# Low parts of the hidden activations of chunks 1 to 3 of both feed-forward layers: written by GpSimd where VectorE wrote them

## The chip, the cores and the metric

The kernel runs on one core of one Trainium2 chip. Its time is the device time of one execution in microseconds (us). Three executions of the kernel before took 1832.42 us in the median (1831.35 to 1832.48). TensorE is called PE in the rows, its weight load PEld, VectorE DVE, ScalarE ACT, GpSimd POOL and the queue that issues the transfers SP.

## The reference

Two blocks follow each other on an activation of 512 tokens by 1024 features in float32: a stick-breaking attention layer and an MLA layer, then an even mixer, a feed-forward layer, a differential attention mixer, a feed-forward layer and a last norm. Of it all, only the feed-forward layers (`L` = 0 and 1) are touched:

```python
def sq_relu_mlp(h, w_up, w_down):
    u = jnp.einsum('btd,df->btf', h, w_up)
    return jnp.einsum('btf,fd->btd', jnp.square(jax.nn.relu(u)), w_down)

for layer in range(DEPTH):            # DEPTH = 2
    ...
    h = h + sq_relu_mlp(rms_norm_2(h, mlp_norm_g[layer]), mlp_w_up[layer], mlp_w_down[layer])
```

Here `w_up` is 1024 by 4096 and `w_down` 4096 by 1024.

## The kernel before

**High and low parts.** Every float32 operand of a matrix product is split in two: a high part, a rounded copy (type fp32r) made by ScalarE, and a low part, the operand minus its high part. A product is then three matmuls: high by high, low by high, high by low. For the weights of ordinary blocks `WH` is the high and `WL` the low part (L269 and L278) of what landed in `WRAW`, which has 2 buffers (`WH` and `WL` have 3). For the hidden activations of a feed-forward layer they are `HIDH` and `HIDL`.

**Four chunks.** A feed-forward layer goes over the 4096 hidden features in four chunks `c` of 1024. In each chunk the up product makes 8 planes of 128 features by 512 tokens, and the down product multiplies them by 8 blocks of `w_down` (`m`), each into its own PSUM bank, and VectorE adds the bank to `X` (L516). Chunk 0 is made in the ordinary way; its low parts are written by GpSimd (L2574, in `mlp_gpsimd`).

**Chunks 1 to 3.** Their up products use Strassen-like block products: 7 half-size products (P1 to P7) instead of 8. One chunk has 4 pairs `p` (two planes of features `p` and `p + 4`), each pair has two halves, which gives 8 slots of 42 matmuls of 256 columns (L2402, L2404, L2405, `fast_pe`). For each slot VectorE forms sums of weight blocks (`fast_sums`, L2331 to L2336), ScalarE the high parts (`fast_high`, L2344) and VectorE the low parts (`fast_low`, L2349) in `G`. When a pair's products are there, ScalarE copies P1 out (`first_act`), VectorE joins the seven products in the one buffer `Q` (`join_first`, L2424, L2428, L2431; `join_last`, L2437), ScalarE takes relu, square and high part (`relu_act`, L2443, L2445, L2447: 128 by 1024 into `HIDH`), and then the low part is made, `HIDL` = `Q` - `HIDH`, 128 by 1024 (`hid_low`, L2451), by VectorE.

**Who waits for the low part.** `join_first` of the next pair writes `Q` again, and so waits for `hid_low` of the pair before. The down product waits for the high and the low part of a plane before its first matmul. It starts with blocks `m` = 0 and 1 on the 6 planes of pairs 0 to 2, and only then takes the planes of pair 3, for both:

```python
ks = (0, 4, 1, 5, 2, 6, 3, 7) if c else tuple(range(8))
...
for m in range(2):
    down(c, m, ks[0:6])
for m in range(2):
    down(c, m, ks[6:8])
```

**What sets the order.** Each engine runs its own hand-written program in order, and semaphores link them. In `mlp_vector` a chunk is a loop of 9 steps `i`, in which the work of several functions is interleaved; `mlp_scalar` has the same loop. The SP queue's order is planned; a load of a weight block into `WRAW` waits for the low part of the block two before, and a load for `fast_sums` waits for the `fast_low` of the slot three before.

Of the kernel before, what the change touches and what calls it, by code (L numbers as in the profile page):

```python
# [45 lines left out]
class Counts:  # L46
# [11 lines left out]
    def inc(self, sem, *keys):  # L58

        self.n[sem] = self.n.get(sem, 0) + 1  # L60
        for key in keys:
            assert self.table.get(key, (sem, self.n[sem])) == (sem, self.n[sem]), (key, sem)
            self.table[key] = (sem, self.n[sem])
        return self.sems.get(sem), 1

    def at(self, *key):

        if not self.sems:
            return None, 0
        sem, n = self.table[key]  # L70
        return self.sems[sem], n
# [65 lines left out]
def program(nc, A, out):  # L137
    ctx = ExitStack()
    with ctx:
# [131 lines left out]
        def split_low(e, w, b, pool):  # L271
            if b >= len(stream) or (b in on_pool) != pool:
                return
            n = stream[b][2]
            if b >= NS:
                w.wait_ge(*at("used", b - NS))
            w.wait_ge(*at("high", b))
            e.tensor_tensor(WL[b % NS][:, 0:n], WRAW[b % NR][:, 0:n], WH[b % NS][:, 0:n].bitcast(F32),  # L278
                            ALU.subtract).then_inc(*inc("s_low_pool" if pool else "s_low", ("low", b)))
# [10 lines left out]
        def after_block(name, m=0):  # L290

            return block[name, m] + NS
# [176 lines left out]
        def factor_vec(e, w, g):  # L469
            s = TMP[:, 1, :]  # L470
            w.wait_ge(*at("sum", g))
            e.tensor_scalar(s, banks["sum", g], 1.0 / DM, EPS, ALU.mult, ALU.add).then_inc(*inc("s_newton", ("mean", g)))
            if g in rn_of:
                w.wait_ge(*at("token sum", g))
                e.tensor_scalar(RN2[:, :], banks["token sum", g][:, 0:NT], 1.0 / DM, EPS, ALU.mult, ALU.add).then_inc(
                    *inc("s_newton", ("token mean", g)))
            w.wait_ge(*at("mean", g))
            w.wait_ge(*at("guess", g))
            newton(e, w, g, "newton", s, RS[:, :], "rs")
# [34 lines left out]
        def add_x(e, w, name, m):  # L514
            w.wait_ge(*at("tile", name, m))
            e.tensor_tensor(X[:, m, :], X[:, m, :], banks[name, m], ALU.add).then_inc(  # L516
                *inc("s_evac", ("evac", name, m)))
# [501 lines left out]
        for h in range(L1_HEADS):  # L1019
            p = halves[h % 2]  # L1020
# [1287 lines left out]
        def flat(x):  # L2308
            return x.rearrange("p s n -> p (s n)")
# [18 lines left out]
        def fast_sums(e, w, L, s):  # L2328
            w.wait_ge(*dma(f"s_raw{s % 3}", L * NF // 3 + s // 3 + 1))
            a21, a11, a12, a22, s1, s3, s2, s4 = (raw_part(s, i) for i in range(8))  # L2330
            e.tensor_tensor(s1, a21, a22, ALU.add).then_inc(*inc("s_fast_sum", ("first sum", L, s)))  # L2331
            e.tensor_tensor(s3, a21, a11, ALU.subtract).then_inc(*inc("s_fast_sum", ("third sum", L, s)))
            w.wait_ge(*at("first sum", L, s))
            e.tensor_tensor(s2, s1, a11, ALU.subtract).then_inc(*inc("s_fast_sum", ("second sum", L, s)))
            w.wait_ge(*at("second sum", L, s))
            e.tensor_tensor(s4, a12, s2, ALU.subtract).then_inc(*inc("s_fast_sum", ("sums", L, s)))  # L2336
# [10 lines left out]
        def fast_low(e, w, L, s):  # L2347
            w.wait_ge(*at("fast high", L, s))
            e.tensor_tensor(flat(G[s % 3][:, 7:14, :]), raw_part(s, 1, 7), flat(G[s % 3][:, 0:7, :]).bitcast(F32),  # L2349
                            ALU.subtract).then_inc(*inc("s_fast_low", ("fast low", L, s)))  # L2350

        def stage_vec(e, w, L, p):
            g = f"mlp{L}"
            w.wait_ge(*at("rs", g))
            for i, k in ((6, p), (4, p + 4)):
                made = e.scalar_tensor_tensor(out=flat(STAGE[p][:, i:i + 2, :]), in0=X[:, k, :], scalar=gain(g)[:, k:k + 1],
                                              in1=RS[:, :], op0=ALU.mult, op1=ALU.mult)
                made.then_inc(*inc("s_staged", *[("plane staged", L, p)] * (i == 4)))

        def plane_mix(e, w, L, p):  # L2360
            S = STAGE[p]
            w.wait_ge(*at("plane staged", L, p))
            e.tensor_tensor(S[:, 0:2, :], S[:, 7:8, :].broadcast_to([128, 2, 256]), S[:, 5:7, :], ALU.subtract).then_inc(
                *inc("s_mixed", ("first mix", L, p)))
            w.wait_ge(*at("first mix", L, p))
            e.tensor_tensor(S[:, 2, :], S[:, 5, :], S[:, 1, :], ALU.subtract).then_inc(
                *inc("s_mixed", ("second mix", L, p)))
            w.wait_ge(*at("second mix", L, p))
            e.tensor_tensor(S[:, 3, :], S[:, 4, :], S[:, 2, :], ALU.subtract).then_inc(*inc("s_mixed", ("mixed", L, p)))
# [64 lines left out]
        def join_last(e, w, L, c, pair):  # L2434
            key = (L, c, pair)
            w.wait_ge(*at("product", *key, "P4"))
            e.tensor_tensor(Q[:, 0:4:3, :], Q[:, 5:7, :], pair_bank(pair, 3), ALU.add).then_inc(  # L2437
                *inc("s_joined", ("joined", *key, 3)))
# [10 lines left out]
        def hid_low(e, w, L, c, p):  # L2449
            w.wait_ge(*at("hid hi", L, c, p))  # L2450
            e.tensor_tensor(flat(HIDL[:, 4 * p:4 * p + 4, :]), flat(Q[:, 0:4, :]),  # L2451
                            flat(HIDH[:, 4 * p:4 * p + 4, :]).bitcast(F32), ALU.subtract).then_inc(
                *inc("s_fast_hid_lo", ("hid lo", L, c, p)))
# [36 lines left out]
        def mlp_vector(e, w, L):  # L2490
            g = f"mlp{L}"
            for m in range(8):
                if m == 0:
                    factor_vec(e, w, g)
                w.wait_ge(*at("tile", ("up", L, 0), m))
                if m > 3:
                    w.wait_ge(*at("hid lo", L, 0, m - 4))
                e.scalar_tensor_tensor(out=TMP[:, m % 4, :], in0=banks[("up", L, 0), m], scalar=0.0, in1=RS[:, :],
                                       op0=ALU.max, op1=ALU.mult).then_inc(*inc("s_evac", ("evac", ("up", L, 0), m)))
                split_low(e, w, after_block(("up", L, 0), m), False)  # L2500
                if 0 < m < 5:
                    stage_vec(e, w, L, m - 1)
            for c in range(4):
                first = 8 * c
                if c:
                    for i in range(9):
                        s = first - 8 + i
                        if i and not i % 2:
                            join_last(e, w, L, c, i // 2 - 1)
                        if 0 < i < 6:  # L2510
                            fast_low(e, w, L, s + 2)
                        if i < 5:
                            fast_sums(e, w, L, s + 3)
                        if i > 5:
                            split_low(e, w, block[("dn", L, c), i - 6], False)
                        if i and not i % 2:
                            hid_low(e, w, L, c, i // 2 - 1)
                        if i % 2:
                            join_first(e, w, L, c, i // 2)
                if c == 3:  # L2520
                    break
                for m in range(8):
                    add_x(e, w, ("dn", L, c), m)
                    if m < 5:
                        split_low(e, w, after_block(("dn", L, c), m), False)
                    if c == 0 and m < 4:
                        plane_low(e, w, L, m)
                    if m > 4:
                        fast_low(e, w, L, first + m - 5)
                    if 3 < m < 7:  # L2530
                        fast_sums(e, w, L, first + m - 4)
            if L == 0:
                close_vec(e, w, ("dn", 0, 3), "mix1")
# [37 lines left out]
        def mlp_gpsimd(e, w, L):  # L2571
            for m in range(8):
                w.wait_ge(*at("hid hi", L, 0, m))
                e.tensor_tensor(hid_plane(m, 1), TMP[:, m % 4, :], hid_plane(m, 0).bitcast(F32),  # L2574
                                ALU.subtract).then_inc(*inc("s_hid_lo", ("hid lo", L, 0, m)))
                if m > 3:
                    plane_mix(e, w, L, m - 4)


        o_slots = [slot for b in range(4) for slot in (("o_q", 2 * b), ("o_k", 2 * b), ("o_q", 2 * b + 1),  # L2580
# [945 lines left out]
```

## Time and profile before

| | |
|---|---|
| median of 3 executions | 1832.42 us (1831.35 to 1832.48) |
| profiled execution, its own time | 1835.86 us |
| its span in the trace | 1834.0 us |
| busy: PE, DVE, ACT, POOL | 98%, 63%, 47%, 25% of the span |
| granted TensorE clock, mean | 0.995 |
| chain of work that ended last | 85% PE, 6% DVE, 4% ACT, 2% POOL |

The shares of busy time are averages over all layers. The chain that ended last is followed back from the last instruction, at each step to what released it; its share by engine says which engine set the end. The stages of interest are the chunks 1 to 3 of the two feed-forward layers, at 968.7 to 1220 us and at 1570.5 to 1822 us of the span. A row of the timeline gives start, duration, engine, line, operation, output and inputs, and in brackets the idle time of its engine before it and who ended it. A row's duration holds a start-up that overlaps the end of the instruction before it, so two rows of one engine overlap a little.

### The profile page before, as it was taken

How to read it: one execution, taken by the hardware profiler on the slowest of the kernel's cores; microseconds unless marked ns; L12 is line 12 of the kernel's file. 1: busy time of each engine (PE TensorE's matmuls, PEld its weight loads, DVE VectorE, ACT ScalarE, POOL GpSimd, SP SyncE). 2: the span in 40 equal slices, each digit the busy share in tenths (PEclk: the TensorE clock that was granted, in tenths of full speed). 3: DMA queues.
4: the chain of work that ended last, by engine and by line, in shares of the span. 5: the costliest groups of instructions: out<-in, count | busy, mean ns of one | idle time of the engine just before them, and what ended most of it. 6: DMA issues, size and time to landing. Idle time of an engine off the chain costs nothing.

```text
span 1834.0 us, 26208 instructions
## 1 busy us (share of the span) xinstructions
PE 1789.8 (98%) x10340; PEld 1460.4 (80%) x10340; DVE 1150.3 (63%) x1861; ACT 866.9 (47%) x1409; POOL 450.9 (25%) x451
## 2 busy tenths in 40 slices
PE   7999999999999999999999999999999999999997
PEld 6877777775678757677879898988888787989896
DVE  5355556575546688854578575765677657858574
ACT  5236665455435465564345252633445434435253
POOL 0035551101311235560140000005678214000000
PEclk9999999999999999999999999999999999999999
DMA  5321111231013411111232322222222123232322
GB/s 177 101 78 49 47 47 58 80 101 50 24 47 100 133 60 34 36 36 58 80 122 86 115 93 104 93 97 83 84 88 76 46 81 127 81 115 92 106 91 80
DMA packets 44521, 149.20 MB, mean 81 GB/s; under 512 B 6000, under 2 KB 6384, under 8 KB 44400
## 3 DMA queue, kind: packets, MB, share of 16 engines
q1 hardware_dynamic: 44400, 147.53, 24.1%
q8 instruction: 83, 1.36, 0.3%
q14 instruction: 38, 0.31, 0.1%
HBM read 139.64 MB, written 2.10 MB: 77 GB/s over the span
## 4 chain that ended last, share of the span: by engine, by line
PE 85%; DVE 6%; ACT 4%; POOL 2%; issue 2%; DMA 1%; POOLq 0%; SPq 0%; DVEq 0%; ACTq 0%
PE BANK L301 18%; PE BANK L303 17%; PE BANK L302 17%; PE BANK L2405 4%; PE BANK L2404 4%; PE BANK L2402 4%; PE BANK L955 3%; PE BANK L688 2%; PE BANK L1739 1%; PE BANK L1720 1%; DMA WRAW<-in_wc 1%; DVE WL L278 1%; PE BANK L1696 1%; PE BANK L1012 1%; PE BANK L2710 1%
## 5 line engine op out<-in xcount | busy, mean ns | idle before, releaser
L269 ACT ACTIVATE WH<-WRAW 128x1024 fp32r<-128x1024 f32 (+1 forms) x214 | 223.0, 1044 | 340.8 <-PE BANK L303 306.0
L278 DVE TENSOR_TENSOR WL<-WRAW,WH 128x1024 fp32r<-128x1024 f32 (+1 forms) x201 | 256.3, 1276 | 138.8 <-ACT WH L269 138.6
L301 PE MATMUL BANK<-HH,WH 128*128 128x512 f32 x664 | 273.1, 411 | 12.1 <-DVE WL L278 9.8
L303 PE MATMUL BANK<-HL,WH 128*128 128x512 f32 x664 | 260.2, 392 | 0.0
L302 PE MATMUL BANK<-HH,WL 128*128 128x512 f32 x664 | 259.9, 391 | 0.0
L301 PE MATMUL BANK<-HIDH,WH 128*128 128x512 f32 (+1 forms) x520 | 201.2, 387 | 1.6 <-issue 1.5
L302 PE MATMUL BANK<-HIDH,WL 128*128 128x512 f32 (+1 forms) x520 | 200.7, 386 | 0.0
L303 PE MATMUL BANK<-HIDL,WH 128*128 128x512 f32 (+1 forms) x520 | 200.7, 386 | 0.0
L2405 PE MATMUL BANK<-HP,G 128*128 128x256 f32 x672 | 190.2, 283 | 0.0
L2404 PE MATMUL BANK<-HP,G 128*128 128x256 f32 x672 | 190.2, 283 | 0.0
L2402 PE MATMUL BANK<-HP,G 128*128 128x256 f32 x672 | 190.1, 283 | 0.0
L516 DVE TENSOR_TENSOR X<-X,BANK 128x512 f32<-128x512 f32 x95 | 65.2, 686 | 167.9 <-PE BANK L303 167.7
L301 PEld LDWEIGHTS BANK<-HH,WH 128*128 128x128 f32 x664 | 125.5, 189 | 46.6 <-issue 22.5
L303 PEld LDWEIGHTS BANK<-HL,WH 128*128 128x128 f32 x664 | 125.2, 189 | 27.1
L302 PEld LDWEIGHTS BANK<-HH,WL 128*128 128x128 f32 x664 | 125.6, 189 | 25.6 <-issue 2.9
L2404 PEld LDWEIGHTS BANK<-HP,G 128*128 128x128 f32 x672 | 129.0, 192 | 0.2
L2402 PEld LDWEIGHTS BANK<-HP,G 128*128 128x128 f32 x672 | 129.0, 192 | 0.2
L2405 PEld LDWEIGHTS BANK<-HP,G 128*128 128x128 f32 x672 | 129.0, 192 | 0.0
L301 PEld LDWEIGHTS BANK<-HIDH,WH 128*128 128x128 f32 x520 | 97.7, 188 | 22.6 <-issue 3.2
L303 PEld LDWEIGHTS BANK<-HIDL,WH 128*128 128x128 f32 x520 | 97.7, 188 | 19.8
L302 PEld LDWEIGHTS BANK<-HIDH,WL 128*128 128x128 f32 x520 | 97.7, 188 | 19.4
L2344 ACT ACTIVATE G<-RAW 128x1792 fp32r<-128x1792 f32 x32 | 54.5, 1703 | 88.3 <-DVE RAW L2336 68.7
(446 smaller groups left out, 3694.2 us busy)
## 6 DMA issues: line engine op xcount, KB each, us to landing
WRAW<-in_w SPq DMA_DIRECT2D x77, 512.0 KB, 3.5
WRAW<-in_wd SPq DMA_DIRECT2D x64, 512.0 KB, 3.5
RAW<-in_wf SPq DMA_DIRECT2D x32, 512.0 KB, 3.6
WRAW<-in_wu SPq DMA_DIRECT2D x16, 512.0 KB, 3.5
TMP<-in_wf SPq DMA_DIRECT2D x16, 512.0 KB, 3.5
WRAW<-in_w0o SPq DMA_DIRECT2D x8, 512.0 KB, 3.5
WRAW<-in_w1o SPq DMA_DIRECT2D x8, 512.0 KB, 3.4
WRAW<-in_wc SPq DMA_DIRECT2D x8, 512.0 KB, 3.5
```

Of the source, the lines that this page charges most:

```text
L269: e.activation(WH[b % NS][:, 0:n], WRAW[b % NR][:, 0:n], ACT.Copy).then_inc(*inc("s_high", ("high", b)))
L278: e.tensor_tensor(WL[b % NS][:, 0:n], WRAW[b % NR][:, 0:n], WH[b % NS][:, 0:n].bitcast(F32), ALU.subtract).then_inc(*inc("s_low_pool" if p ...
L301: e.matmul(dst, ah, bh, start=first and i == 0, stop=False)
L302: e.matmul(dst, al, bh, start=False, stop=False)
L303: made = e.matmul(dst, ah, bl, start=False, stop=last and i == len(sets) - 1)
L516: e.tensor_tensor(X[:, m, :], X[:, m, :], banks[name, m], ALU.add).then_inc(*inc("s_evac", ("evac", name, m)))
L688: made = e.matmul(l0_bank(h, bk)[:, c0 + 128 * (jj - j):c0 + size[j]], ntri if jj == j else nones, nlf[:, h % 2, col[jj]:col[jj] + size[jj ...
L955: made = e.matmul(bank[:, c], a, b, start=(i == 0), stop=(i == len(sets) - 1), skip_group_check=True)
L2344: e.activation(flat(G[s % 3][:, 0:7, :]), raw_part(s, 1, 7), ACT.Copy).then_inc(*inc("s_fast_high", ("fast high", L, s)))
L2402: e.matmul(dst, wh[:, a, cols], hi, start=half == 0 and j not in started, stop=False, skip_group_check=True)
L2404: e.matmul(dst, wl[:, a, cols], hi, start=False, stop=False, skip_group_check=True)
L2405: made = e.matmul(dst, wh[:, a, cols], lo, start=False, stop=half == 1 and i == 1, skip_group_check=True)
```

## The change

`hid_low` is called from `mlp_gpsimd` instead of `mlp_vector`. The function is the same, with the same wait and the same semaphore, and the low part is the same subtraction of 128 by 1024 elements. 24 instructions move: 2 layers, 3 chunks, 4 pairs.

```diff
@@ mlp_vector: loop over the 9 steps i of a chunk
                         if i > 5:
                             split_low(e, w, block[("dn", L, c), i - 6], False)
-                        if i and not i % 2:
-                            hid_low(e, w, L, c, i // 2 - 1)
                         if i % 2:
                             join_first(e, w, L, c, i // 2)
@@ mlp_gpsimd: behind the loop over chunk 0
                 if m > 3:
                     plane_mix(e, w, L, m - 4)
+            for c in range(1, 4):
+                for p in range(4):
+                    hid_low(e, w, L, c, p)
```

On VectorE, at pair 0 of chunk 1 of layer 0, the program's order changes like this (difference of before and after; L2334 and L2336 are the last sums of a slot, L2349 the `fast_low` of the next):

```order
 L2334 TENSOR_TENSOR TMP<-TMP 128x256
 L2336 TENSOR_TENSOR TMP<-TMP 128x256
-L2451 TENSOR_TENSOR HIDL<-Q,HIDH 128x1024
 L2349 TENSOR_TENSOR G<-TMP,G 128x1792
 L2331 TENSOR_TENSOR RAW<-RAW 128x256
```

The `hid_low` between them is gone, and `fast_low` follows the sums.

On VectorE, at the end of the same chunk (pairs 2 and 3), before; L278 is the low part of a block of the down weights:

```order
L2437 TENSOR_TENSOR Q<-Q,BANK 128x2x256
L278 TENSOR_TENSOR WL<-WRAW,WH 128x1024
L2451 TENSOR_TENSOR HIDL<-Q,HIDH 128x1024
L278 TENSOR_TENSOR WL<-WRAW,WH 128x1024
L2424 TENSOR_TENSOR Q<-Q,BANK 128x2x256
L2428 TENSOR_TENSOR Q<-Q,BANK 128x512
L2431 TENSOR_TENSOR Q<-Q,BANK 128x256
L2437 TENSOR_TENSOR Q<-Q,BANK 128x2x256
L278 TENSOR_TENSOR WL<-WRAW,WH 128x1024
L2451 TENSOR_TENSOR HIDL<-Q,HIDH 128x1024
L516 TENSOR_TENSOR X<-X,BANK 128x512
```

and in the changed kernel:

```order
L2437 TENSOR_TENSOR Q<-Q,BANK 128x2x256
L278 TENSOR_TENSOR WL<-WRAW,WH 128x1024 x2
L2424 TENSOR_TENSOR Q<-Q,BANK 128x2x256
L2428 TENSOR_TENSOR Q<-Q,BANK 128x512
L2431 TENSOR_TENSOR Q<-Q,BANK 128x256
L2437 TENSOR_TENSOR Q<-Q,BANK 128x2x256
L278 TENSOR_TENSOR WL<-WRAW,WH 128x1024
L516 TENSOR_TENSOR X<-X,BANK 128x512
```

The `hid_low` of pair 2 stood between two weight splits, and that of pair 3 was the last of the chunk; both are gone from VectorE.

On GpSimd, behind the last `plane_mix` (L2363 to L2369) of layer 0, where the next work was that of the attention layer after it (L3091, one line later in the changed kernel):

```order
L2363 TENSOR_TENSOR STAGE<-STAGE 128x512
L2366 TENSOR_TENSOR STAGE<-STAGE 128x256
L2369 TENSOR_TENSOR STAGE<-STAGE 128x256
L2451 TENSOR_TENSOR HIDL<-Q,HIDH 128x1024 x12
L3092 TENSOR_TENSOR TMP<-TMP,ROPE 128x512
L3099 TENSOR_TENSOR OS<-TMP,OS 128x512
```

The 12 instructions of a layer stand in a row in GpSimd's program, with nothing of its other work between them.

## Rows read from the trace of the kernel before

**Rows 1.** Stretches: length, busy (count) of PE PEld DVE ACT POOL, clock, DMA, GB/s
```profile
968.70:1009.10 40.40, 40.40 (x338) 40.36 (x338) 33.27 (x46) 22.73 (x22) 0.00 (x0) 1.00 0.24 81
...
1738.20:1822.00 83.80, 83.80 (x547) 77.09 (x547) 52.14 (x69) 37.32 (x41) 0.00 (x0) 1.00 0.20 70
```

**Rows 2.** Groups of instructions by line and form: busy us, mean ns, idle before
```profile
L2451 DVE TENSOR_TENSOR HIDL<-Q,HIDH 128x1024 fp32r<-128x1024 f32 x24 | 29.4, 1224 | 26.1 <-ACT HIDH L2447 26.1
...
L278 POOL TENSOR_TENSOR WL<-WRAW,WH 128x1024 fp32r<-128x1024 f32 x6 | 14.3, 2390 | 4.2 <-ACT WH L269 4.2
```

**Rows 3.** Timeline of VectorE, chunk 1 of layer 0
```profile
985.04 1.22 DVE L2451 TENSOR_TENSOR HIDL<-Q,HIDH 128x1024 fp32r<-128x1024 f32 x1
986.89 2.03 DVE L2349 TENSOR_TENSOR G<-TMP,G 128x1792 fp32r<-128x1792 f32 x1 [0.63 <-ACT G L2344]
...
997.99 2.03 DVE L2349 TENSOR_TENSOR G<-RAW,G 128x1792 fp32r<-128x1792 f32 x1 [0.63 <-ACT G L2344]
...
1005.77 1.23 DVE L2451 TENSOR_TENSOR HIDL<-Q,HIDH 128x1024 fp32r<-128x1024 f32 x1 [2.18 <-ACT HIDH L2447]
1006.91 1.22 DVE L278 TENSOR_TENSOR WL<-WRAW,WH 128x1024 fp32r<-128x1024 f32 x1
1008.04 0.68 DVE L2424 TENSOR_TENSOR Q<-Q,BANK 128x512 f32<-128x512 f32 x1
...
1013.89 1.23 DVE L2451 TENSOR_TENSOR HIDL<-Q,HIDH 128x1024 fp32r<-128x1024 f32 x1 [2.18 <-ACT HIDH L2447]
```

**Rows 4.** Timeline of ScalarE, chunk 1 of layer 0
```profile
983.93 1.06 ACT L2447 ACTIVATE HIDH<-Q 128x1024 fp32r<-128x1024 f32 x1
...
1002.49 1.06 ACT L2443 ACTIVATE Q<-Q 128x1024 f32<-128x1024 f32 x1 [3.32 <-DVE Q L2437]
...
1012.79 1.06 ACT L2447 ACTIVATE HIDH<-Q 128x1024 fp32r<-128x1024 f32 x1
```

**Rows 5.** Timeline of TensorE: first plane and first plane of pair 3, down product
```profile
1009.07 0.40 PE L301 MATMUL BANK<-HIDH,WH 128*128 128x512 f32 x1
...
1017.25 0.39 PE L301 MATMUL BANK<-HIDH,WH 128*128 128x512 f32 x1
```

**Rows 6.** Timeline, chunk 3 of layer 1: low part of pair 3, its first matmul
```profile
1783.51 1.23 DVE L2451 TENSOR_TENSOR HIDL<-Q,HIDH 128x1024 fp32r<-128x1024 f32 x1 [2.18 <-ACT HIDH L2447]
...
1786.74 0.39 PE L301 MATMUL BANK<-HIDH,WH 128*128 128x512 f32 x1
```

**Rows 7.** Timeline, GpSimd and VectorE on two SBUF inputs at the same time
```profile
926.72 1.29 POOL L2574 TENSOR_TENSOR HIDL<-TMP,HIDH 128x512 fp32r<-128x512 f32 x1
...
926.88 2.21 DVE L278 TENSOR_TENSOR WL<-WRAW,WH 128x1024 fp32r<-128x1024 f32 x1 [2.31 <-ACT WH L269]
...
936.27 1.66 POOL L2369 TENSOR_TENSOR STAGE<-STAGE 128x256 f32<-128x256 f32 x1
...
937.25 2.57 DVE L2380 TENSOR_TENSOR HP<-STAGE,HP 128x1792 fp32r<-128x1792 f32 x1
...
1304.49 2.35 POOL L3098 TENSOR_TENSOR OS<-TMP,OS 128x512 fp32r<-128x512 f32 x1
...
1304.49 1.21 DVE L278 TENSOR_TENSOR WL<-WRAW,WH 128x1024 fp32r<-128x1024 f32 x1
```

**Rows 8.** Timeline: who starts how long after whom, and GpSimd's 128 by 1024
```profile
892.12 0.63 ACT L2544 ACTIVATE HIDH<-TMP 128x512 fp32r<-128x512 f32 x1
...
892.84 1.30 POOL L2574 TENSOR_TENSOR HIDL<-TMP,HIDH 128x512 fp32r<-128x512 f32 x1 [55.70 <-ACT HIDH L2544]
...
149.77 0.74 POOL L920 TENSOR_TENSOR LH<-SCR,LH 128x256 fp32r<-128x256 f32 x1 [0.23 <-DVE LH L798]
...
150.56 0.73 PE L688 MATMUL BANK<-LH,TRI 128*128 128x512 f32 x2 [0.32 <-POOL LH L920]
...
1279.26 2.37 POOL L278 TENSOR_TENSOR WL<-WRAW,WH 128x1024 fp32r<-128x1024 f32 x1
```

**Rows 9.** The page's transfer issues: KB each, median us to landing
```profile
WRAW<-in_wd SPq DMA_DIRECT2D x64, 512.0 KB, 3.5
```

## Prediction

> **What bounds the kernel now.** I read the busy time by stretch first. In the first block-product stretch of chunk 1 TensorE is busy for all of its 40.40 us at the full clock, and in the last one, chunk 3 of layer 1 with its down product, for all of its 83.80 us, while GpSimd does nothing in either [rows 1]. So in these chunks TensorE alone sets the time: relief of VectorE gives nothing back, and the change can only cost where it makes TensorE wait. The groups then give the sizes: the 24 `hid_low` take 1.22 us each on VectorE, and the nearest GpSimd operation, the same subtraction of 128 by 1024 with the same types, takes 2.39 us in the mean [rows 2], 2.37 where nothing stands in its way [rows 8].
>
> The timelines show the margins. VectorE runs `hid_low` of pair 0 at 985.04, then waits 0.63 us for ScalarE's high part before `fast_low` at 986.89; 11.10 us later, at 997.99, stands the same picture for pair 1. `hid_low` of pair 2 starts at 1005.77, a weight split (L278) follows at 1006.91 and `join_first` of pair 3 right behind it at 1008.04; `hid_low` of pair 3 starts at 1013.89 [rows 3]. In between ScalarE waits for VectorE (3.32 us before the relu of pair 2) and takes three passes of 1.06 us; the high part of pair 3 is ready at 1012.79 + 1.06 = 1013.85 [rows 4]. TensorE starts the down product at 1009.07 and comes to the first plane of pair 3 after 36 matmuls, at 1017.25 [rows 5]. That is the only deadline that is near: the low part of pair 3 is ready at 1013.89 + 1.23 = 1015.12, 2.13 us before. The six chunks repeat this within 0.02 us (start of `hid_low` to deadline 3.36 us), but for the last, with 3.23 us [rows 6].
>
> **The change, step by step.** *Removed:* 24 times 1.2 us on VectorE. At pairs 0 and 1 this frees nothing, since `fast_low` behind it waits for ScalarE, whose order does not change; the 1.2 us turn into waiting. At pairs 2 and 3 VectorE waits for ScalarE's high part anyway. Worth to TensorE: 0.
>
> *Added on GpSimd:* 2.37 us in place of 1.22. It starts 892.84 - (892.12 + 0.63) = 0.09 us after ScalarE's end, where VectorE took 1013.89 - 1013.85 = 0.04, and TensorE starts 150.56 - (149.77 + 0.74) = 0.05 us after a GpSimd end [rows 3, 4, 8]. By itself: 1013.85 + 0.09 + 2.37 + 0.05 = 1016.36, still 0.89 us ahead of 1017.25. Nothing on GpSimd's queue waits behind it: it is idle in these stretches [rows 1].
>
> *What it does to VectorE.* The trace has cases of both engines subtracting SBUF tensors at once [rows 7]. GpSimd's L2574 ran from 926.72 to 928.01; VectorE's split, started at 926.88, took 2.21 us, not 1.22, and ended at 929.09, 1.08 us after GpSimd. GpSimd's L2369 ended at 937.93; VectorE's L2380, 128 by 1792 like `fast_low`, took 2.57 us and ended at 939.82, 1.89 us after. The other way round, GpSimd's L3098 at 1304.49, beside a VectorE split that kept its 1.21 us, took 2.35 us in place of about 1.3. So of two such operations the later one stands still until the first has ended, and then needs 1.08 us (split) or 1.89 us (`fast_low`). `hid_low`, the splits and `fast_low` all read two SBUF tensors. With that:
> - Pair 0: high part ready at 983.93 + 1.06 = 984.99; GpSimd from 985.08 to 987.45. `fast_low` wants 986.89, ends at 987.45 + 1.89 = 989.34 where it ended at 988.92: VectorE is 0.42 us late, and all that hangs on it.
> - Pair 1: same picture, 11.10 + 0.42 later: GpSimd ends at 998.97, `fast_low` at 1000.86 where it was 1000.02: 0.84 late.
> - Pair 2: its high part was ready at 1005.73, now 1006.57; GpSimd from 1006.66 to 1009.03. The weight split behind it, whose high part ScalarE has 1.06 us after, at about 1007.6, ends at 1009.03 + 1.08 = 1010.11 where it ended at 1008.13: 1.98 late. `join_first` of pair 3 is right behind it, so 1.98 late too.
> - Pair 3: high part at 1013.85 + 1.98 = 1015.83, GpSimd 1015.92 to 1018.29, TensorE at 1018.34 in place of 1017.25: it stands 1.09 us. In the last chunk, 3.36 - 3.23 = 0.13 more, 1.22 us.
>
> The lateness is lost again before the next chunk: in the down product VectorE and ScalarE wait for TensorE. **Sum:** 5 x 1.09 + 1.22 = 6.67 us.
>
> The rule in the Trainium skill is in SBUF — State Buffer, section SBUF: two separate sides: VectorE operations with two SBUF inputs and GpSimd operations share a port pair, and whoever starts first has it for the whole instruction while the other blocks. The traced rows above agree. Taken literally, with the blocked instruction paying its whole duration behind the other (1.22 and 2.03 in place of 1.08 and 1.89), the latenesses would be 0.56, 1.12 and 2.40, the stalls 1.51 and 1.64, and the sum 9.2 us in place of 6.67. I go by the rows, which show that the start-up overlaps.
>
> *Bounds of what no row shows.* How soon TensorE is at its pace after such a stop: from 0 to one matmul step of 8.18 / 36 = 0.23 us per chunk, as the next weights may only be loaded then. The row of rows 8 shows the matmul 0.05 us after the release, so I take 0; the other end is 8.0 us. That the three latenesses do not add up, and only the last counts, is the lower end, worked out below.
>
> *What covers the rest.* Queues: the load of the down block m = 2 waits for the split that is 0.84 late, and its high part stands on ScalarE ahead of pair 3's relu. The split ends at about 1003.6 + 0.84 = 1004.4 (it runs right before the relu of pair 2, from about 1002.4); 3.5 us for the transfer [rows 9] and 1.06 for the high part end at 1009.0, and the relu starts at about 1012.5: cover 3.5 us; beyond it each us would be one more of stall. The late `fast_low` has some 3 us: that of slot 7 ends at 1000.86, and TensorE needs it one eighth of the 40.3 us before 1009.07, at 1004.0. The split for m = 1 ends at 1010.11 and is needed 18 matmuls after 1009.07, at 1013.2. The low part of pair 2, at 1009.03, is needed after 12 matmuls, at 1011.8.
>
> **The rivals.**
> - *GpSimd runs beside VectorE and the stops in rows 7 have another cause.* Then only the 1.15 us stay, 0.89 us ahead of the deadline (0.7 if `join_first` of pair 3 waits for GpSimd's end at 1008.24 rather than 1008.04). TensorE never waits: 0 us, 1832.4. This is the one on the other side, not slower; it decides where the lateness at pair 3 stays under 0.89 us. Against it stand three rows with three different pairs of lines. Chance 8%.
> - *The latenesses of pairs 0 and 1 are made good on the way* (some wait of ScalarE takes them up), and only pair 2's counts: GpSimd from 1005.82 to 1008.19, split ended at 1009.27, 1.14 late, stall 0.25 us (0.38 in the last): 1.6 us, 1834.0. For it speaks the 0.63 us wait at `fast_low`; against, that this wait is for an operation which itself follows VectorE's joins. Chance 10%.
> - *The blocked operation pays in full*, or TensorE needs its step more: 9.2 us, 1841.6. Chance 7%.
> - *Forecast:* 6.7 us, up to 8.0. Chance 75%.
>
> **The numbers.** The profiled execution took 1835.86 us itself, with 1.9 us around its span of 1834.0: the sum gives 1842.5 for such a one. It lies 3.4 us above the median of 1832.42, and against that median the forecast is 1832.42 + 6.67 = 1839.1 us. The likeliest case alone reaches from 1838 to 1840.5. For 8 in 10 I take the second and third rivals in, 1834.0 to 1842.0, and leave the first out. 0.2% is 3.7 us, about what a measurement of this kernel tells from no change. Slower by more takes a stall of 0.6 us per chunk: forecast and third rival, less something for an error in the chain of latenesses, 0.79. Within it: the first two rivals and that error, 0.18. Faster needs a wait of TensorE that the change shortens, and there is none in these stretches: 0.03.
>
> **What the profile after would show.** `hid_low` on GpSimd at 2.37 us, 24 times. VectorE's `fast_low` behind pairs 0 and 1 at about 2.5 us in place of 2.03; the weight split beside pair 2 at about 2.4 us in place of 1.22. ScalarE's high part of pair 3 2.0 us later against TensorE's start of the down product. TensorE idle for about 1.1 us, six times, at the 37th matmul of the down product of chunks 1 to 3, released by GpSimd's L2451. The forecast is wrong if these waits are missing (first rival), a quarter as long (second), or if TensorE also waits in the block products, which would mean that `fast_low` is later than its 3 us.

## The result and the profile after

The changed kernel took 1840.61 us in the median of 4 executions (1840.39 to 1844.49), the kernel before 1832.45 us (1831.35 to 1835.41) beside it. The ratio is 1.0047, with an interval of 1.0029 to 1.0065: slower by 8.2 us (5.3 to 11.9 by the interval). A second series beside other runs of before (1832.4 us) gave 1840.78 us, a ratio of 1.0046 (1.0033 to 1.0058).

The page of the changed kernel: its span, the busy rows of the engines, and the shares of the chain that ended last.

```profile
span 1838.6 us, 26204 instructions
...
PE 1786.5 (97%) x10336; PEld 1456.5 (79%) x10340; DVE 1137.4 (62%) x1837; ACT 866.6 (47%) x1409; POOL 507.4 (28%) x475
...
PE 72%; DVE 13%; ACT 6%; POOL 4%; issue 3%; DMA 1%; POOLq 0%; SPq 0%; DVEq 0%; ACTq 0%
```

VectorE has 24 instructions less, and the chain that ended last now goes 13% over it where it was 6%, and 4% over GpSimd where it was 2%. An engine was relieved and yet stands more in the chain. Its busy time fell by 12.9 us only (1150.3 to 1137.4), where 29.4 us of `hid_low` went; the next groups show what came in their place. The span grew by 4.6 us only, since the profiled execution of before was itself 3.4 us above its median: its granted TensorE clock was 0.97 in the mean from 1400 to 1500 us, where it was 1.00 in the changed kernel, and from the first block product of layer 0 to that of layer 1 it took about 3 us more than other executions without such a dip (601.77 us against 598.68 in the copy run below).

The waits of TensorE, the longest three in total (total us, times, longest):

```profile
PE BANK L301 <- DVE WL L278: 11.1, 4, 10.0
PE BANK L301 <- POOL HIDL L2451: 6.7, 6, 1.1
PE BANK L688 <- POOL LH L920: 4.8, 9, 1.4
```

The second row is new: six waits of 1.1 us for the low part from GpSimd, one per chunk. The others were there before. One stretch, from the first block product of chunk 1 of layer 0 to that of chunk 2 (length, then busy of PE, PEld, DVE, ACT and POOL, clock, DMA, GB/s), in the kernel before and in the changed kernel:

```profile
968.75:1052.61 83.86, 83.86 (x529) 76.35 (x528) 56.00 (x76) 35.68 (x33) 0.00 (x0) 1.00 0.29 101
```

```profile
968.06:1053.29 85.23, 84.12 (x529) 76.29 (x528) 53.66 (x72) 35.69 (x33) 9.60 (x4) 1.00 0.28 100
```

The same 529 matmuls at the same full clock take 1.37 us more. The four chunks that another one follows repeat this to 0.04 us (83.86 before, 85.23 to 85.27 after). The two last chunks lose it in their down product, from its first matmul to the first of the work behind it: 50.39 us where it was 48.99 in layer 0, and 43.82 where it was 42.42 in layer 1. The six together are 8.33 us, so the whole loss lies there.

Groups by line and form (busy us, mean ns, idle before), in the kernel before:

```profile
L278 DVE TENSOR_TENSOR WL<-WRAW,WH 128x1024 fp32r<-128x1024 f32 x195 | 251.3, 1289 | 138.8 <-ACT WH L269 138.6
L2349 DVE TENSOR_TENSOR G<-RAW,G 128x1792 fp32r<-128x1792 f32 x32 | 64.7, 2021 | 16.0 <-ACT G L2344 16.0
```

and in the changed kernel, which answers to [rows 2]:

```profile
L278 DVE TENSOR_TENSOR WL<-WRAW,WH 128x1024 fp32r<-128x1024 f32 x195 | 259.7, 1332 | 153.9 <-ACT WH L269 153.7
L2349 DVE TENSOR_TENSOR G<-RAW,G 128x1792 fp32r<-128x1792 f32 x32 | 68.3, 2136 | 25.1 <-ACT G L2344 25.1
L2451 POOL TENSOR_TENSOR HIDL<-Q,HIDH 128x1024 fp32r<-128x1024 f32 x24 | 57.6, 2399 | 445.2 <-ACT HIDH L2447 445.2
```

The low part takes 2.40 us on GpSimd, not 1.22. `fast_low` and the weight splits were not touched, yet `fast_low` takes 2.14 us in the mean where it took 2.02, and the splits together 8.4 us more.

The timelines of GpSimd, VectorE and TensorE in chunk 1 of layer 0 of the changed kernel (up to here this execution runs 0.70 us ahead of the one shown for before: `fast_low` of pair 0 starts at 986.19 and not 986.89; so 0.70 is taken off [rows 3, 4, 5] when they are compared):

```profile
984.38 2.41 POOL L2451 TENSOR_TENSOR HIDL<-Q,HIDH 128x1024 fp32r<-128x1024 f32 x1 [47.14 <-ACT HIDH L2447]
986.19 2.48 DVE L2349 TENSOR_TENSOR G<-TMP,G 128x1792 fp32r<-128x1792 f32 x1 [1.77 <-ACT G L2344]
...
995.94 2.41 POOL L2451 TENSOR_TENSOR HIDL<-Q,HIDH 128x1024 fp32r<-128x1024 f32 x1 [9.15 <-ACT HIDH L2447]
997.75 2.48 DVE L2349 TENSOR_TENSOR G<-RAW,G 128x1792 fp32r<-128x1792 f32 x1 [1.77 <-ACT G L2344]
...
1006.03 2.41 POOL L2451 TENSOR_TENSOR HIDL<-Q,HIDH 128x1024 fp32r<-128x1024 f32 x1 [7.68 <-ACT HIDH L2447]
1006.93 2.59 DVE L278 TENSOR_TENSOR WL<-WRAW,WH 128x1024 fp32r<-128x1024 f32 x1 [3.12 <-ACT WH L269]
1009.44 0.68 DVE L2424 TENSOR_TENSOR Q<-Q,BANK 128x512 f32<-128x512 f32 x1
...
1014.18 1.06 ACT L2447 ACTIVATE HIDH<-Q 128x1024 fp32r<-128x1024 f32 x1
1015.32 2.36 POOL L2451 TENSOR_TENSOR HIDL<-Q,HIDH 128x1024 fp32r<-128x1024 f32 x1 [6.88 <-ACT HIDH L2447]
...
1015.88 0.39 PE L301 MATMUL BANK<-HIDH,WH 128*128 128x512 f32 x1
1017.83 0.47 PE L301 MATMUL BANK<-HIDH,WH 128*128 128x512 f32 x1 [1.11 <-POOL HIDL L2451]
1018.60 0.39 PE L301 MATMUL BANK<-HIDH,WH 128*128 128x512 f32 x1
```

This is the forecast chain. `fast_low` behind pairs 0 and 1 takes 2.48 us, and ends 1.88 us after GpSimd; the split beside pair 2 takes 2.59 us and ends 1.08 us after GpSimd. The lateness of VectorE is 0.45 us after pair 0 (end 988.67 against 988.22), 0.91 after pair 1 (1000.23 against 999.32) and 2.09 after the split (1009.52 against 1007.43). The high part of pair 3 is ready at 1015.24, 2.09 late, and TensorE starts on pair 3 1.95 us after the plane before instead of 0.68 us, and takes 0.77 us for the next step. The waiting shows on the bracket of one row of TensorE only; the lateness behind it is seen in durations of rows that have grown and in no bracket of VectorE at all.

### The profile page after: what moved, and what is told of

The parts are those of the page before. It is cut to its first block, busy times and chain, and to the rows that moved or that the text cites. A ratio compares the mean times of both kernels' runs of the same rounds, so it can differ in the third digit from the quotient of the medians.

```text
span 1838.6 us, 26204 instructions
## 1 busy us (share of the span) xinstructions
PE 1786.5 (97%) x10336; PEld 1456.5 (79%) x10340; DVE 1137.4 (62%) x1837; ACT 866.6 (47%) x1409; POOL 507.4 (28%) x475
## 4 chain that ended last, share of the span: by engine, by line
PE 72%; DVE 13%; ACT 6%; POOL 4%; issue 3%; DMA 1%; POOLq 0%; SPq 0%; DVEq 0%; ACTq 0%
PE BANK L301 18%; PE BANK L303 17%; PE BANK L302 17%; DVE G L2349 3%; PE BANK L955 3%; PE BANK L688 2%; ACT G L2344 2%; PE BANK L1739 1%; PE BANK L1720 1%; PE BANK L1696 1%; PE BANK L1012 1%; PE BANK L2736 1%; DVE WL L278 1%; PE BANK L673 1%; PE BANK L2711 1%
## 5 line engine op out<-in xcount | busy, mean ns | idle before, releaser
L278 DVE TENSOR_TENSOR WL<-WRAW,WH 128x1024 fp32r<-128x1024 f32 (+1 forms) x201 | 264.8, 1318 | 154.9 <-ACT WH L269 154.7
L2451 POOL TENSOR_TENSOR HIDL<-Q,HIDH 128x1024 fp32r<-128x1024 f32 x24 | 57.6, 2399 | 445.2 <-ACT HIDH L2447 445.2
```

## The experiments

The theory: a VectorE operation with two inputs in SBUF and a GpSimd operation that reads SBUF do not run together; what VectorE loses so adds up along its program to the high part of pair 3, where TensorE has the only near deadline. Rival A: only GpSimd's longer duration at pair 3 counts. Rival B: every moved instruction costs the same share. The length of a chunk, from its first block product to that of the next, is read off the timeline of TensorE in each run; in before it is 83.86 us. The median of before, run beside each experiment, is given with its time.

### Which pairs are on GpSimd

Three kernels give some pairs back to VectorE, at their old places, with a semaphore of their own:

```diff
-                        if i % 2:
+                        if i and not i % 2 and i // 2 - 1 in ON_VEC:
+                            hid_low(e, w, L, c, i // 2 - 1)
+                        if i % 2:
...
                 for p in range(4):
-                    hid_low(e, w, L, c, p)
+                    if p not in ON_VEC:
+                        hid_low(e, w, L, c, p)
```

`ON_VEC = (2,)`:

> The low part of pair 2 is back on VectorE, those of pairs 0, 1 and 3 stay on GpSimd. Theory (the port is held, and the latenesses of VectorE add up along the chain to the high part of pair 3): the weight split beside pair 2 is no longer held up, so 1.2 us of the 2.1 us of lateness go, pair 3 comes 0.9 us late and TensorE stands 0 to 0.2 us per chunk: +0 to +1.5 us against the kernel before. Rival A (only GpSimd's longer duration at pair 3 counts): as the changed kernel, +8 us. Rival B (each moved instruction costs the same share, 0.34 us): 18 of 24, +6 us.

Measured: 1833.64 us beside 1832.3, ratio 1.0010 (1.0001 to 1.0019), +1.3 us; chunks of 84.09 us, +0.23. The theory holds. The trace has no wait of TensorE on `HIDL` any more; the 0.23 us show only as steps of 0.80 and 0.77 us in place of 0.68 at the deadline, since the low part ends just then, 0.02 us ahead of it.

`ON_VEC = (0, 1)`:

> The low parts of pairs 0 and 1 are back on VectorE, those of pairs 2 and 3 stay on GpSimd. Theory: only the weight split beside pair 2 is held up, 1.2 us of lateness; TensorE stands 0.3 us per chunk and needs some 0.2 us more to be at its pace: +1.7 to +3 us. Rival A: +8 us. Rival B (equal shares): 12 of 24, +4 us.

Measured: 1835.13 us, ratio 1.0016 (1.0007 to 1.0025), +2.8 us; chunks of 84.36 us, +0.50. TensorE waits six times, 1.4 us in all; the next rows are from its timeline in this run:

```profile
1015.54 0.39 PE L301 MATMUL BANK<-HIDH,WH 128*128 128x512 f32 x1
1016.62 0.47 PE L301 MATMUL BANK<-HIDH,WH 128*128 128x512 f32 x1 [0.24 <-POOL HIDL L2453]
1017.39 0.40 PE L301 MATMUL BANK<-HIDH,WH 128*128 128x512 f32 x1
```

The idle time is 0.24 us, but the two steps are 1.08 and 0.77 us and not 0.68: with 0.01 us of the step after them TensorE loses 0.50 us. So a stop costs about 0.25 us beside the idle time that its row names, in the changed kernel too (1.37 against 1.11). Of it, 0.16 us are no further cost but a matter of the rows: a matmul follows the one before after 0.23 us, but its row lasts 0.39, and the idle time is counted from the end of the row. A start that is late by less than 0.16 us so gets no bracket at all. The other 0.10 us are the step to the next plane.

`ON_VEC = (3,)`:

> The low part of pair 3 is back on VectorE, those of pairs 0 to 2 stay on GpSimd. Theory: all the lateness is there (high part of pair 3 2.1 us late), but VectorE needs 1.2 us where GpSimd needed 2.4, so that the low part is ready about when TensorE comes to it: TensorE stands 0 to 0.2 us per chunk, +0 to +1.5 us. Rival A: +0. Rival B: 18 of 24, +6 us.

Measured: 1833.95 us, ratio 1.0009 (1.0000 to 1.0018), +1.7 us; chunks of 84.04 to 84.09 us, +0.2. The six losses add up to 1.2 us, inside what was expected; the median lies 0.15 us above it, with an interval that reaches from 0 to 3.3 us. Here 18 of the 24 instructions are on GpSimd and VectorE is as late as in the changed kernel, but its own 1.23 us at pair 3 make good for it.

`ON_VEC = (0, 1, 2)`:

> Only the low part of pair 3 on GpSimd, those of pairs 0 to 2 on VectorE. Theory: nothing is held up before it, and GpSimd's 2.4 us end 0.8 us before TensorE comes to pair 3: chunks of 83.86 us and +0 us. Rival A (GpSimd's own duration at pair 3 makes the loss): +8 us.

Measured: 1832.96 us beside 1832.4, ratio 1.0002 (0.9993 to 1.0011); chunks of 83.86 us. This decides against rival A: GpSimd's longer duration at pair 3, alone, costs nothing (it ends 0.91 us ahead of the deadline). Rival B falls with the same runs, since 18 moved instructions cost 1.3 or 1.7 us and not 6.

### The deadline

All low parts stay on GpSimd; the down product of chunks 1 to 3 takes three planes of block 2 first:

```diff
+                if c:
+                    down(c, 2, ks[0:3])
                 for m in range(2):
                     down(c, m, ks[6:8])
-                for m in range(2, 7 if L and c == 3 else 8):
+                if c:
+                    down(c, 2, ks[3:8])
+                for m in range(3 if c else 2, 7 if L and c == 3 else 8):
                     down(c, m, ks)
```

> All 24 low parts on GpSimd as in the changed kernel, but the down product of chunks 1 to 3 takes the first three planes of block m = 2 before the planes of pair 3 of blocks 0 and 1: the deadline of pair 3 is 9 matmuls, 2.0 us, later. Theory: VectorE is held up as before, but TensorE no longer waits: +0 us against the kernel before. If the loss came from anything else than this one wait (a slower TensorE stream, waits in the block products), it stays: +8 us.

Measured: 1832.05 us beside 1832.3, ratio 1.0000 (0.9992 to 1.0009); chunks of 83.86 us. `fast_low` still takes 2.14 us:

```profile
L2349 DVE TENSOR_TENSOR G<-RAW,G 128x1792 fp32r<-128x1792 f32 x32 | 68.3, 2135 | 25.1 <-ACT G L2344 25.1
```

VectorE is held up just as much and the time is that of before. The whole loss goes through this one wait. The control is the same order of the down product with the low parts on VectorE:

> The kernel before (low parts on VectorE) with the later deadline for pair 3 in the down product. A control: TensorE had no wait there, so all theories expect +0 us against the kernel before. If it were faster, the equality of the kernel with the later deadline and GpSimd would be a gain that covers a loss.

Measured: 1832.01 us beside 1832.69, ratio 0.9999 (0.9989 to 1.0009). The later deadline is no gain by itself, so it does not cover a loss.

### The split that is in the way

All low parts on GpSimd; VectorE's weight split for m = 1 goes behind the joins of pair 3:

```diff
-                        if i > 5:
-                            split_low(e, w, block[("dn", L, c), i - 6], False)
+                        if i == 6:
+                            split_low(e, w, block[("dn", L, c), 0], False)
+                        if i == 8:
+                            for m in (1, 2):
+                                split_low(e, w, block[("dn", L, c), m], False)
```

> All 24 low parts on GpSimd, but VectorE makes the low part of down block m = 1 behind the joins of pair 3 instead of ahead of them. Theory: the 0.9 us of lateness from pairs 0 and 1 stay; at pair 2 the split is no longer in the way, but join_first of pair 3 still waits for GpSimd's low part of pair 2 (it writes Q), so of the 2.1 us of lateness 1.2 to 1.3 are left. TensorE is held 0.4 to 0.6 us per chunk: +2.5 to +3.5 us against the kernel before. If the held split were not what makes pair 3 late, as the changed kernel: +8 us.

Measured: 1836.20 us beside 1832.4, ratio 1.0021 (1.0012 to 1.0030), +3.8 us (2.2 to 5.5 by the interval); chunks of 84.46 to 84.49 us, +0.60 to 0.63. That is at the upper end of the 0.4 to 0.6 us expected for a chunk, and the time is 0.3 us above the +3.5 expected. The held split makes over half of the loss, not all. GpSimd and VectorE in this run:

```profile
1007.15 2.42 POOL L2451 TENSOR_TENSOR HIDL<-Q,HIDH 128x1024 fp32r<-128x1024 f32 x1 [7.69 <-ACT HIDH L2447]
...
1009.70 0.69 DVE L2424 TENSOR_TENSOR Q<-Q,BANK 128x512 f32<-128x512 f32 x1 [4.76 <-PE BANK L2405]
```

`join_first` starts 0.13 us after GpSimd's end at 1009.57. The row names TensorE as releaser, but the wait is for several semaphores; GpSimd's is the one that fits, because `Q` must be free: in before the same join starts 1.03 us ahead of the first matmul of the down product [rows 3, 5], here 0.23 us behind it (1009.47), so its products were there long before.

The runs so far line up by one number, the end of the low part of pair 3 against the first matmul of the down product (chunk 1 of layer 0, us):

| low parts on GpSimd | low part of pair 3 ends at | TensorE starts pair 3 at | the chunk is longer by |
|---|---|---|---|
| none (before) | 6.05 | 8.18 | 0 |
| pair 3 | 7.27 | 8.18 | 0 |
| pairs 0 to 2 | 8.14 | 8.28 | 0.18 |
| pairs 0, 1 and 3 | 8.16 | 8.31 | 0.23 |
| pairs 2 and 3 | 8.44 | 8.59 | 0.50 |
| all, split behind the joins | 8.51 | 8.66 | 0.60 |
| all (the change) | 9.31 | 9.46 | 1.37 |

In every row with a loss the matmul starts 0.14 or 0.15 us after the low part ends, whichever engine made it, and about 0.1 us more are lost behind it.

### What of GpSimd's operation holds VectorE up

The kernel before, with an operation on GpSimd in layer 1 that nothing waits for; it overwrites a rotation table that is no longer used, so the output is the same:

```diff
+            if L:
+                for c in range(1, 4):
+                    for p in range(3):
+                        w.wait_ge(*at("hid hi", L, c, p))
...
+                        e.tensor_copy(flat(ROPE[:, :, :]), flat(ROPE[:, :, :])).then_inc(*inc("s_extra", ("extra", c, p)))
```

(or `memset`, or `tensor_tensor` with `ROPE` as both inputs and `ALU.subtract`).

> The kernel before, with 9 GpSimd instructions more in layer 1, which nothing waits for: a memset of 128 by 1024 into a table that is no longer used, each started by the high part of pairs 0, 1 and 2. It reads nothing in SBUF. If only operations that read SBUF meet on the port, VectorE's rows keep 2.02 us (fast_low) and 1.22 us (split) and the time stays (+0 us). If any GpSimd operation holds it, the rows grow as in the run with two inputs.

> The same with a GpSimd copy of 128 by 1024 in place of the memset: one SBUF input. If one input is enough to hold the port, VectorE's fast_low and split behind it stand still until it has ended: rows above 2.02 and 1.22 us if the copy ends after they want to start. If two are needed, they stay.

> The same with a GpSimd subtraction of 128 by 1024, two SBUF inputs. Theory: VectorE's low part starts 0.05 us earlier and goes first, GpSimd waits for it (3.5 us in place of 2.4) and then holds up fast_low by 1.4 us at pairs 0 and 1 (3.4 us in place of 2.02) and the weight split by 2.1 us at pair 2; the low part of pair 3 comes 4.9 us late and TensorE stands about 3 us in each chunk of layer 1: +9 us, though nothing waits for any of the 9 instructions. If the loss of the change came from waiting for GpSimd's result and not from the port, +0 us.

One execution each: 1830.76, 1831.57 and 1840.03 us, beside 1832.69. One execution cannot settle a difference of 1 or 2 us; the answer is in the rows of chunk 1 of layer 1, pair 0. Memset:

```profile
1581.72 1.23 DVE L2451 TENSOR_TENSOR HIDL<-Q,HIDH 128x1024 fp32r<-128x1024 f32 x1
1581.75 0.95 POOL L2584 MEMSET ROPE<- 128x1024 f32 x1 [48.07 <-ACT HIDH L2447]
```

Copy:

```profile
1582.55 1.23 DVE L2451 TENSOR_TENSOR HIDL<-Q,HIDH 128x1024 fp32r<-128x1024 f32 x1
1582.58 2.10 POOL L2584 COPY ROPE<-ROPE 128x1024 f32<-128x1024 f32 x1 [48.04 <-ACT HIDH L2447]
1584.40 2.15 DVE L2349 TENSOR_TENSOR G<-TMP,G 128x1792 fp32r<-128x1792 f32 x1 [0.63 <-ACT G L2344]
```

Subtraction:

```profile
1585.54 1.23 DVE L2451 TENSOR_TENSOR HIDL<-Q,HIDH 128x1024 fp32r<-128x1024 f32 x1
1585.59 2.93 POOL L2584 TENSOR_TENSOR ROPE<-ROPE 128x1024 f32<-128x1024 f32 x1 [48.07 <-ACT HIDH L2447]
1587.40 3.00 DVE L2349 TENSOR_TENSOR G<-TMP,G 128x1792 fp32r<-128x1792 f32 x1 [0.63 <-ACT G L2344]
```

The memset, which reads nothing, begins and ends (1582.70) inside VectorE's subtraction (to 1582.95); both run at once, and `fast_low` and the splits behind it keep 2.02 and 1.22 us. The copy ends at 1584.68, 0.90 us after VectorE's end, and `fast_low` ends 1.87 us after that: one input is enough. The subtraction ends at 1588.52, and `fast_low` at 1590.40, 1.88 us after, 0.97 us late. TensorE then waits in all three chunks of layer 1 (chunks of 85.6 us), though no instruction waits for GpSimd's result. So the latenesses come from the two engines holding each other up, without any wait in the program, and need nobody who waits for what GpSimd makes. The three chunks lose 1.78, 1.75 and 1.92 us, less than the 3 us expected: the subtraction took 1.75 us after VectorE's end where I had reckoned with 2.3, from the durations of `hid_low` itself. Why a subtraction with one tensor as both inputs is quicker was not tried. The 5.45 us of the chunks are not the whole 7.3 us of this one execution: like the profiled one of before it has a granted clock of 0.97 from 1400 to 1500 us, and takes 601.67 us from the first block product of layer 0 to that of layer 1.

That VectorE's side must read SBUF with two inputs was not tried by a run, but the trace of before has a case of an operation with one input in SBUF and one in PSUM:

```profile
933.10 2.27 POOL L2363 TENSOR_TENSOR STAGE<-STAGE 128x512 f32<-128x512 f32 x1
934.96 0.69 DVE L516 TENSOR_TENSOR X<-X,BANK 128x512 f32<-128x512 f32 x1 [0.74 <-PE BANK L303]
```

It starts 0.41 us before GpSimd's end and keeps its 0.69 us.

The Trainium skill, SBUF — State Buffer, section SBUF: two separate sides, states that a VectorE operation with two SBUF inputs meets only such GpSimd operations as read SBUF. The three traces agree: VectorE's row keeps 1.23 us beside the memset, and grows from 2.02 to 2.15 behind the copy and to 3.00 behind the subtraction.

## Why the prediction was right

- *TensorE bounds, and relief of VectorE is worth 0.* Right. VectorE's idle time before `fast_low` grew from 24.0 to 37.6 us in both forms together, as said, and no wait of TensorE became shorter in these chunks.
- *GpSimd alone would not be late (0.89 us ahead).* Right: with pair 3 alone on GpSimd the chunks stay at 83.86 us.
- *The latenesses 0.42, 0.84 and 1.98 us.* Right in mechanism; measured 0.45, 0.91 and 2.09. The lateness is gone again before the next chunk, as said: the high part of pair 0 ends 24.06 or 24.07 us before the down product in each of the six. GpSimd took 2.41 us beside VectorE and not 2.37 us, three times. The steps 1.89 and 1.08 us after GpSimd's end, read off two other lines, came out as 1.88 and 1.08. The split's row, 2.59 us, is longer than the "about 2.4" given for the profile after; the prediction's own steps (from about 1007.6 to 1010.11) make it 2.5.
- *The stall, 1.09 us.* Measured 1.38. This is the term that was sized too small: 0.11 is the lateness; 0.10 is the release, 0.15 us from GpSimd's end (1017.68) to the matmul (1017.83), where I took 0.05 from a stop in another stage; 0.10 is the way back to TensorE's pace, which I had bounded by one step of 0.23 and taken as 0; and 0.02 go off again, since GpSimd started 0.08 and not 0.09 us after ScalarE and took 2.36 and not 2.37. That the idle time named by the row is 1.11, close to the forecast 1.09, is chance: it is not the whole stall.
- *0.13 us more in the last chunk.* Wrong: it lost 1.40 us where the other five lost 1.37 to 1.41. Its high part of pair 3 came 6.88 us after the first matmul of the down product, as in the others (6.87 to 6.89), while in before it had come 0.14 us later than there. Why that lateness is gone is open.
- *The sum.* It is 8.33 us in place of 6.67. The measured 1840.6 lies inside the range, but a little above the upper end of the likeliest case's own (1840.5).
- *The rule taken literally, 9.2 us.* The stall of 1.38 us could pass for halfway, but the rows that it speaks of decide: the split ended 1.08 us after GpSimd and not 1.22. I read that as the start-up that overlaps; the rest of the loss came at TensorE.
- *Rivals.* That GpSimd runs beside VectorE is refuted by the durations of 2.48 and 2.59 us. That the latenesses of pairs 0 and 1 are made good is refuted: with these two pairs back on VectorE the loss falls from 8.4 to 2.8 us, and with pair 2 back it falls to 1.3. The price of that rival was also too small: with pairs 0 and 1 on VectorE, which is its case, TensorE loses 0.50 us per chunk and not 0.25, by the same release and way back. Neither part reaches far alone, because the 0.9 us of margin have to be used up first.
- *The covers.* No wait in the block products and none for a transfer appeared.

## What to carry to other kernels

In this kernel, moving an elementwise operation from VectorE to GpSimd did not free VectorE for the operation's time, because VectorE's next operations read SBUF with two inputs: 1.2 us of work go, and 0.5 us (`fast_low`) to 1.4 us (the split) of standing still come, which no wait in the program shows. Look for the growth in the durations of untouched rows, follow the lateness to the next deadline of the bounding engine, and compare it with the margin there; the first part of it is free, and all beyond it is paid. The margin is to be counted up to the release, here 0.15 us ahead of the matmul. Where the order of the bounding engine can be changed, a later deadline (here 9 matmuls of another block first) is the cheap cure, though here it only brought back the old time.

## What the runs showed of the hardware

- A GpSimd memset of 128 by 1024 (0.95 us) runs beside a VectorE subtraction that keeps its 1.23 us; a GpSimd copy with a single SBUF input does not, and took 2.10 us, of which 1.2 were VectorE's. A VectorE operation with one input in SBUF and one in PSUM kept its 0.69 us beside a GpSimd operation that reads SBUF.
- TensorE started 0.15 us after GpSimd's end in this place (0.14 after VectorE's), its first matmul then took 0.47 and not 0.39 us, and the step to the next plane 0.77 and not 0.68. Idle time as named by the row was 1.11 us where 1.37 were lost.
- A low part that ended 0.02 to 0.04 us before TensorE's turn still cost 0.2 us per chunk, with no wait on TensorE's row: by the release it was late (steps of 0.77 to 0.80 us). One that ended 0.91 us before cost nothing.
